# The rotation tables of a scanned state layer: GpSimd starts them behind the first norm, and VectorE makes its first pair behind the lower half of h

## The chip, the cores and the metric

The kernel runs on one core of a Trainium2 chip. The metric is the device time of one execution in microseconds (us), the median of several runs. A core has five engines with a queue each: PE (TensorE, matrix products into PSUM), DVE (VectorE), ACT (ScalarE), POOL (GpSimd), and SP (SyncE, which here issues nearly all the transfers). Each works its queue in order and waits on semaphores.

## The reference, cut to what matters

Two networks of two layers each run one after the other on x, 256 tokens by 1024 features, in float32. The change lies in the first layer of the first network: a norm, one projection that gives u (for a state-space layer) and q, k, v (for attention), and the linear recurrence over the 256 tokens.

```python
h = modulate(rms_norm(x, norm_g[layer, 0]), sh1, sc1)
proj = h @ ab_w_in[i]                 # 1024 -> 512 (u) + 3 * 512 (q, k, v)
y_ssm = s5_mixer(u, ...)              # 32 groups x 64 complex states
...
# s5_mixer: x_t = a * x_(t-1) + (B u)_t for every complex state, a = exp(lambda * dt)
_, _, xr, xi = lax.associative_scan(combine, (a_full_re, a_full_im, bu_re, bu_im), axis=1)
y = einsum(xr, c_re) - einsum(xi, c_im) + d_skip * uf
```

The kernel turns the complex recurrence into a real one: it multiplies B u by e^(-i*theta*t), runs two real scans with the magnitude of a, and multiplies by e^(i*theta*t). The cosines and sines of theta*t are the rotation tables.

## The kernel before, in words

The 32 x 64 = 2048 states lie in ST = 16 tiles of 128 partitions. The tables `e_re` and `e_im` have 16 tiles of 256 tokens each. A call of `e_pair(v, link, g)` (lines 491 to 502) makes two tiles of both, with six operations of 128x512 on engine `v`: four products and a difference and a sum, all between tiles in SBUF (two SBUF inputs each), from the small tables `e1` and `e2`. The tables have eight pairs. GpSimd makes pairs 4 to 7 (tiles 8 to 15) in its first loop (lines 725 to 728), which waits for `powers_ready` alone, that is for `e1` and `e2`. VectorE makes pair 0 behind `x_scaled(0)`, pair 1 behind the split of the third weight chunk, and pairs 2 and 3 behind tiles 2 and 4 of the scan. GpSimd's tables are first read by tile 8 of the scan, far behind: VectorE waits there for `e_ready`.

Every weight comes as a chunk of 128x2048 into one of three buffers. ACT rounds it (`w_hi`, L750), DVE makes the rest (`w_lo`, L1338), and PE multiplies three products for each pair of tiles (L2231), 48 products a chunk here. ACT's `w_hi(q)` waits for PE to have used chunk q-3; the load of chunk q waits for ACT and DVE to have split chunk q-3.

The order of work at the start, as each queue has it:

- PE: 16 pieces of the modulation's weights as they land (L2182), `x_turn(0)` (16 transposes of the scaled x into PSUM, L2105), `pm_turn(1)` (L2189), then chunk 0 of `ab_in`, which follows `h_ready` pair by pair; `bu(0)` and `bu(1)` (L2286); then for c = 1 to 7 chunk c, `bu(c+1)`, and from c = 2 on `y_of(c-2)` (L2299). `bu(j)` needs `bu_used` of tile j-2, because two banks take turns.
- DVE: `x_scaled(0)` (L1507, L1516), `e_pair` 0, `w_lo(0)`, `first_mod_out` (L1492, waits for `pm_turn(1)`), `x_gains(0)` (L1523), `x_lower(0)` (L1539, L1540; the lower half of h), `w_lo(1)` and `w_lo(2)`, `e_pair` 1; then for c = 0 to 7: `w_lo(c+3)`, `ssm_tile(c)` (L1614 to L1631).
- ACT: `w_hi(0)`, `x_upper(0)` (L792, L794, waits for the gains), `w_hi(1)`, `w_hi(2)`; then for each c the copy out of chunk c (L904) and `w_hi(c+3)`.
- SP: the pieces, chunks 0 and 1, and when all 16 pieces are used chunks 2 to 5; then, behind a wait for `h_ready` of the whole first norm, four transfers of attention biases, then chunks 6 and 7 and what follows. Behind `w_lo(10)`, the last split of this stretch, come the later pieces of the modulation.

`h_ready` is counted by `x_lower`; `H[1]` = 4 is its value when the first norm's h is complete. In a scan tile L1614 and L1615 read a PSUM bank and a table; L1617, L1618, the two scans L1620, L1629 and L1631 read SBUF alone, with two inputs each. The second of them, L1615, releases `bu_used`.

Of the kernel before, what the change touches and what calls it, by code (L numbers as in the profile page):

```python
# [255 lines left out]
def build(nc, A, out):  # L256
    with ExitStack() as ctx:
# [5 lines left out]
        def sem(name):  # L263
            if name not in names:
                names[name] = ctx.enter_context(nc.semaphore(name))
            return names[name]
# [172 lines left out]
        def chunks(name, n):  # L439
            Q[name] = sum(k for _, k in stream)  # L440
            stream.append((name, n))
# [5 lines left out]

        MB = {1: 0, 4: MOD_BLOCKS}
        NQ = sum(k for _, k in stream)

        raw_landed = [sem(f"raw_landed{i}") for i in range(SLOTS)]
# [39 lines left out]
        def e_pair(v, link, g):  # L491

            j = slice(2 * g, 2 * g + 2)
            a, b = ([e[:, i, j, :].unsqueeze(k).broadcast_to([P, 2, 16, 16]) for i in range(2)] for e, k in ((e1, 3), (e2, 2)))
            er, ei = (t[:, j, :].rearrange("p j (a b) -> p j a b", b=16) for t in (e_re, e_im))
            part = e_part[g >= E_POOL]
            v.tensor_tensor(er, a[0], b[0], ALU.mult)
            link(v.tensor_tensor(part, a[1], b[1], ALU.mult))
            link(v.tensor_tensor(er, er, part, ALU.subtract))
            v.tensor_tensor(ei, a[0], b[1], ALU.mult)  # L500
            link(v.tensor_tensor(part, a[1], b[0], ALU.mult))
            return v.tensor_tensor(ei, ei, part, ALU.add)
# [48 lines left out]
        SQ, UPPER, H, SCALES = [0], [0], [0], [0]  # L551
# [20 lines left out]
        def _(sp):  # L572
# [10 lines left out]
            def load_mod(m, i=None):  # L583

                more = 0 if i is None else 6 * i
                buf, landed, _, n = MOD_HALF[m]
                sp.wait_ge(sem("mod_used"), MOD_SLOTS + m - n + 1 + more)
                src = A["mod_stream"][bass.ds(m + more, 1)].rearrange("o p (k n) -> (o p) k n", k=DT // 2)
                sp.dma_start(buf, src).then_inc(landed, 16)
# [128 lines left out]
        @block.gpsimd  # L718
        def _(pool):
            done = Count(sem("pool_chain"))  # L720

            def link(ins):
                pool.wait_ge(done.sem, done.on(ins))

            pool.wait_ge(sem("powers_ready"), 1)
            for g in range(E_POOL, ST // 2):
                e_pair(nc.gpsimd, link, g).then_inc(sem("e_ready"), 1)
                pool.wait_ge(sem("e_ready"), g - E_POOL + 1)
            for j in range(8, ST):
                pool.wait_ge(sem("scan_done"), j - 7)  # L730
                pool.wait_ge(*((sem("state_ready"), j - 1) if j >= 10 else (sem("ssm_y_done"), j - 1)))
                nc.gpsimd.tensor_tensor(by_sin[j % 2], rot_b, e_im[:, j, :].unsqueeze(1).broadcast_to([P, 2, T]), ALU.mult)\
                    .then_inc(sem("sin_part"), 1)
            pool.wait_ge(sem("h_ready"), H[7])
            pool.wait_ge(sem("mod_turned"), 2 * MOD_BLOCKS)
            for v in (q_head, k_head):
                nc.gpsimd.memset(v[32:64, 1::2, :], 0.0).then_inc(sem("heads_zeroed"), 1)
# [588 lines left out]
        def _(dve):  # L1326
            chain = Count(sem("dve_chain"))

            def link(ins):
                dve.wait_ge(chain.sem, chain.on(ins))  # L1330
# [9 lines left out]
            def lo_upto(q):  # L1340
                while nxt[0] <= min(q, NQ - 1):
                    lo(nxt[0])
                    nxt[0] += 1
# [165 lines left out]
            def x_scaled(n):  # L1509

                if n:
                    dve.wait_ge(sem("h_ready"), H[n])
                for t in range(2):
                    x_recip(n, t)
                    for fh in range(2):
                        nc.vector.tensor_scalar(x_at(hf_tok, t, fh), x_at(x, t, fh), x_rstd[:, t:t + 1], None, ALU.mult)\  # L1516
                            .then_inc(sem("x_scaled"), 1)
# [81 lines left out]
            dve.wait_ge(sem("x_landed"), 16)  # L1599
            dve.wait_ge(sem("c_ready"), 1)  # L1600
            x_scaled(0)
            link(e_pair(nc.vector, link, 0))
            lo_upto(0)
            first_mod_out(0, 2)
            x_gains(0)
            x_lower(0)
            lo_upto(2)
            link(e_pair(nc.vector, link, 1))

            def ssm_tile(j):  # L1610
                dve.wait_ge(sem("bu_ready"), j + 1)
# [1177 lines left out]
```

## Time and profile before

| what | value |
| --- | --- |
| median of 3 runs | 1541.3 us (1537.97 to 1543.39) |
| the profiled execution | 1540.02 us, of which the span 1538.2 us |
| granted TensorE clock, mean | 0.969 |
| busy: PE, DVE, ACT, POOL | 1437.3, 1128.9, 772.6, 51.5 us |
| share of the chain that ended last: PE, DVE, ACT, DMA, issue | 73%, 12%, 5%, 5%, 4% |

The span is the profiled part of the execution; 1.8 us lie around it. The chain is followed back from the last instruction, at each step to what released it. A share of busy time is an average over the whole span; the change touches only the first 9% of it, up to some 135 us.

### The profile page before, as it was taken

What the parts mean: (1) busy time and instruction counts of PE and PEld (TensorE: products, weight loads), DVE (VectorE), ACT (ScalarE), POOL (GpSimd) and SP (SyncE); (2) the same over time, 40 slices, a digit from 0 to 9 for tenths busy, and PEclk for the clock granted to TensorE, in tenths of its full rate; (3) what the DMA queues carried; (4) which work ended last, traced back from release to release, by engine and by line L of the source; (5) the groups of instructions that cost most, each with busy time, mean ns of one, the idle gap of its engine ahead of it and who ended that gap; (6) DMA issues with size and microseconds to landing.
All of it is one profiled execution on the core that took longest, in us unless ns stands there. A gap on an engine that the chain in (4) does not pass through costs nothing.

```text
span 1538.2 us, 24906 instructions
## 1 busy us (share of the span) xinstructions
PE 1437.3 (93%) x9469; PEld 1201.6 (78%) x9483; DVE 1128.9 (73%) x1680; ACT 772.6 (50%) x1090; POOL 51.5 (3%) x38
## 2 busy tenths in 40 slices
PE   5598989999988999999999889999999999999998
PEld 1585458899966668999979755799997877799997
DVE  7999756988874465998985467586667859676666
ACT  3332356555554355555555567555455542455554
POOL 2600200000000000000001000000000000000000
PEclk9598999999989999999998999999999999999999
DMA  9332944988859944998833400455554533345551
GB/s 356 136 126 89 334 172 198 354 319 306 310 198 384 373 192 188 355 361 314 337 147 113 134 14 5 149 178 178 194 188 169 187 110 137 110 164 191 177 199 61
DMA packets 58061, 315.65 MB, mean 205 GB/s; under 512 B 7012, under 2 KB 8525, under 8 KB 33857
## 3 DMA queue, kind: packets, MB, share of 16 engines
q1 hardware_dynamic: 53826, 303.30, 53.3%
q10 hardware_dynamic: 4158, 11.30, 2.3%
q8 instruction: 52, 0.85, 0.2%
q14 instruction: 25, 0.20, 0.0%
HBM read 311.85 MB, written 1.15 MB: 203 GB/s over the span
## 4 chain that ended last, share of the span: by engine, by line
PE 73%; DVE 12%; ACT 5%; DMA 5%; issue 4%; SPq 0%; ACTq 0%; DVEq 0%; POOL 0%
PE bank L2231 61%; DMA raw<-in_stream 2%; PE bank L2490 2%; DMA arena<-in_mod_later 2%; ACT w_hi L750 1%; DVE w_lo L1338 1%; PE bank L2105 1%; DVE hf L1552 1%; DVE h_lo L1540 1%; ACT hf L1255 1%; PE bank L2299 1%; PE bank L2182 1%; PE bank L2286 1%; PE bank L2123 1%; ACT hf L792 1%
## 5 line engine op out<-in xcount | busy, mean ns | idle before, releaser
L1338 DVE TENSOR_TENSOR w_lo<-raw,w_hi 128x2048 fp32r<-128x2048 f32 x186 | 426.3, 2293 | 176.8 <-ACT w_hi L750 175.6
L2231 PE MATMUL bank<-h_hi,w_hi 128*128 128x256 f32 x1800 | 519.9, 289 | 18.3 <-DVE h_lo L1540 16.7
L2231 PE MATMUL bank<-h_lo,w_hi 128*128 128x256 f32 x1800 | 513.3, 285 | 0.0
L2231 PE MATMUL bank<-h_hi,w_lo 128*128 128x256 f32 x1800 | 513.1, 285 | 0.0
L750 ACT ACTIVATE w_hi<-raw 128x2048 fp32r<-128x2048 f32 x186 | 355.8, 1915 | 138.7 <-PE bank L2231 114.4
L2231 PEld LDWEIGHTS bank<-h_hi,w_hi 128*128 128x128 f32 x1800 | 349.4, 194 | 19.3 <-DVE h_lo L1540 9.6
L2231 PEld LDWEIGHTS bank<-h_lo,w_hi 128*128 128x128 f32 x1800 | 349.5, 194 | 2.3 <-issue 0.7
L2231 PEld LDWEIGHTS bank<-h_hi,w_lo 128*128 128x128 f32 x1800 | 349.4, 194 | 0.0
L1755 DVE SCALAR_TENSOR_TENSOR arena<-bank,par,arena 128x255 f32<-128x255 f32 (+1 forms) x264 | 109.1, 475 | 111.5 <-ACT arena L987 79.1
L2231 PE MATMUL bank<-w_hi,a_hi 128*128 128x512 f32 x368 | 146.4, 398 | 10.9 <-DVE a_lo L1780 10.1
L2231 PE MATMUL bank<-w_hi,a_lo 128*128 128x512 f32 x368 | 144.5, 393 | 0.0
L2231 PE MATMUL bank<-w_lo,a_hi 128*128 128x512 f32 x368 | 144.4, 392 | 0.0
L987 ACT ACTIVATE arena<-bank,par 128x256 f32<-128x256 f32 x88 | 44.8, 560 | 139.8 <-PE bank L2231 139.8
L1366 DVE SCALAR_TENSOR_TENSOR arena<-arena,silu_c 128x384 f32<-128x384 f32 (+1 forms) x192 | 104.3, 613 | 0.0
L2231 PE MATMUL bank<-w_hi,h_hi 128*128 128x512 f32 (+1 forms) x224 | 87.1, 389 | 5.8 <-DVE hf L1552 3.0
L2231 PEld LDWEIGHTS bank<-w_hi,a_hi 128*128 128x128 f32 x368 | 69.8, 190 | 28.1 <-DVE w_lo L1338 11.1
L2231 PE MATMUL bank<-w_hi,h_lo 128*128 128x512 f32 (+1 forms) x224 | 84.7, 378 | 0.0
L2231 PE MATMUL bank<-w_lo,h_hi 128*128 128x512 f32 (+1 forms) x224 | 84.6, 378 | 0.0
L2231 PEld LDWEIGHTS bank<-w_lo,a_hi 128*128 128x128 f32 x368 | 69.7, 189 | 15.1
L2231 PEld LDWEIGHTS bank<-w_hi,a_lo 128*128 128x128 f32 x368 | 69.9, 190 | 13.1
L1005 ACT ACTIVATE a_hi<-arena 128x512 fp32r<-128x512 f32 x44 | 27.8, 632 | 59.5 <-DVE arena L1776 59.4
L2231 PEld LDWEIGHTS bank<-w_hi,h_hi 128*128 128x128 f32 x224 | 42.7, 191 | 19.0 <-issue 11.1
(327 smaller groups left out, 1705.2 us busy)
## 6 DMA issues: line engine op xcount, KB each, us to landing
raw<-in_stream SPq DMA_DIRECT2D x186, 1024.0 KB, 5.0
arena<-in_mod_stream SPq DMA_DIRECT2D x64, 768.0 KB, 7.6
arena<-in_mod_later SPq DMA_DIRECT2D x48, 512.0 KB, 9.1
raw<-in_mod_pe SPq DMA_DIRECT2D x36, 512.0 KB, 6.3
arena<-in_mod_pe SPq DMA_DIRECT2D x12, 512.0 KB, 12.1
sq<-row_store ACTq DMA_DIRECT2D x7, 512.0 KB, 3.7
sq<-in_bias SPq DMA_DIRECT2D x8, 256.0 KB, 6.8
x<-in_x_t ACTq DMA_DIRECT2D x1, 1024.0 KB, 9.0
```

Of the source, the lines that this page charges most:

```text
L750: nc.scalar.activation(w_hi[s][:], raw[s][:], ACT.Copy).then_inc(hi_done, 1)
L792: nc.scalar.activation(hf[:, k, :], turned(n, k), ACT.Identity, **by).then_inc(sem("full_ready"), 1)
L987: ins = nc.scalar.activation(gate_c[:, e, :], half(4, e), ACT.Identity, scale=par[:, bass.ds(wb[center] + 2 * s + e, 1)], bias=par[:, bass ...
L1005: nc.scalar.activation(slot_hi(q), act_f, ACT.Copy)\
L1255: nc.scalar.activation(mla_s(h, t), bank[u % 4][:], ACT.Exp, bias=small[:, k + 1:k + 2], scale=MLA_SCALE, accum_out=small[:, k + 2:k + 3]) ...
L1338: nc.vector.tensor_tensor(w_lo[s][:], raw[s][:], w_hi[s][:].bitcast(F32), ALU.subtract).then_inc(lo_done, 1)
L1366: ins = nc.vector.scalar_tensor_tensor(parts[e], buf[:, kt % 4, :], silu_c[:, c0 + kt:c0 + kt + 1], parts[e], ALU.mult, ALU.add)
L1540: ins = nc.vector.tensor_tensor(v["parts"][1][:, k, :], hf[:, k, :], up.bitcast(F32), ALU.subtract)
L1552: ins = nc.vector.tensor_tensor(part, acc[:], row_at(gate_rows[gate], fh), ALU.mult)
L1755: ins = nc.vector.scalar_tensor_tensor(o, src, par[:, bass.ds(w[tap] + 2 * s + e, 1)], o, ALU.mult, ALU.add)
L2231: ins = nc.tensor.matmul(out_, l, r, start=first and n == 0, stop=last and n == 2, **kw)
L2490: ins = nc.tensor.matmul(bank[2 * part + ft][:], dft[:, part, t, ft * P:(ft + 1) * P], sources[part][:, t, 512 * s_:512 * s_ + 512], start ...
```

## The change

GpSimd waits for the first norm's h (`h_ready` at `H[1]`) before it begins its four pairs. VectorE's pair 0 moves from behind `x_scaled(0)` to directly ahead of pair 1, behind `x_lower(0)` and `w_lo(2)`. No operation is added or removed but GpSimd's wait.

```diff
             pool.wait_ge(sem("powers_ready"), 1)
+            pool.wait_ge(sem("h_ready"), H[1])
             for g in range(E_POOL, ST // 2):
                 e_pair(nc.gpsimd, link, g).then_inc(sem("e_ready"), 1)
...
             x_scaled(0)
-            link(e_pair(nc.vector, link, 0))
             lo_upto(0)
             first_mod_out(0, 2)
             x_gains(0)
             x_lower(0)
             lo_upto(2)
-            link(e_pair(nc.vector, link, 1))
+            for g in range(2):
+                link(e_pair(nc.vector, link, g))
```

## Rows read from the trace of the kernel before

**Rows 1.** The chain that ended last: start us, us, engine, tile, line.

```profile
69.33 8.33 PE bank L2231 x48
79.46 5.95 PE bank L2231 x48
...
123.67 5.96 PE bank L2231 x48
130.14 1.91 ACT w_hi L750
132.07 2.29 DVE w_lo L1338
```

**Rows 2.** Timeline of DVE, 30 to 63 us: start us, us, line, operation, tiles.

```profile
30.22 2.38 DVE L1516 TENSOR_SCALAR hf<-x,small 128x512 f32<-128x512 f32 x2
...
35.13 1.54 DVE L497 TENSOR_TENSOR arena<-arena 128x512 f32<-128x512 f32 x1
...
42.96 1.43 DVE L502 TENSOR_TENSOR arena<-arena 128x512 f32<-128x512 f32 x1
44.42 3.02 DVE L1338 TENSOR_TENSOR w_lo<-raw,w_hi 128x2048 fp32r<-128x2048 f32 x1
47.37 0.16 DVE L1492 TENSOR_TENSOR mod<-bank,par 128x16 f32<-128x16 f32 x1
47.56 1.02 DVE L1523 SCALAR_TENSOR_TENSOR gains<-mod,par 128x8 f32<-128x8 f32 x1
...
60.91 2.58 DVE L1540 TENSOR_TENSOR h_lo<-hf,h_hi 128x256 fp32r<-128x256 f32 x2
```

**Rows 3.** Timeline of DVE, 67 to 81 us.

```profile
67.81 0.68 DVE L497 TENSOR_TENSOR arena<-arena 128x512 f32<-128x512 f32 x1
...
71.91 2.29 DVE L1338 TENSOR_TENSOR w_lo<-raw,w_hi 128x2048 fp32r<-128x2048 f32 x1
...
74.72 0.68 DVE L1615 TENSOR_TENSOR arena<-bank,arena 128x512 f32<-128x512 f32 x1
...
78.14 0.69 DVE L1631 TENSOR_TENSOR arena<-arena 128x512 f32<-128x512 f32 x1
80.19 2.29 DVE L1338 TENSOR_TENSOR w_lo<-raw,w_hi 128x2048 fp32r<-128x2048 f32 x1 [1.36 <-ACT w_hi L750]
```

**Rows 4.** Timeline of POOL; 24 table operations from 30.07 to 63.20 us.

```profile
30.07 1.06 POOL L497 TENSOR_TENSOR arena<-arena 128x512 f32<-128x512 f32 x1 [29.61 <-DVE arena L1460]
...
45.38 3.19 POOL L502 TENSOR_TENSOR arena<-arena 128x512 f32<-128x512 f32 x1
...
61.86 1.34 POOL L502 TENSOR_TENSOR arena<-arena 128x512 f32<-128x512 f32 x1
142.56 1.71 POOL L732 TENSOR_TENSOR arena<-arena 128x512 f32<-128x512 f32 x1 [79.36 <-DVE arena L1620]
```

**Rows 5.** DVE lines over the whole span: shortest, median and longest of one in ns.

```profile
L1516 DVE TENSOR_SCALAR hf<-x,small x32: 478/485/1306, 30.2 to 1340.7; 128x512 f32<-128x512 f32 x32
L1540 DVE TENSOR_TENSOR h_lo<-hf,h_hi x64: 424/426/1501, 49.9 to 1347.2; 128x256 fp32r<-128x256 f32 x64
```

**Rows 6.** Timeline of ACT, 38 to 56 us.

```profile
48.62 1.02 ACT L792 ACTIVATE hf<-bank,mod,gains 128x256 f32<-128x256 f32 x2 [12.53 <-DVE gains L1523]
...
53.58 0.63 ACT L794 ACTIVATE h_hi<-bank,mod,gains 128x256 fp32r<-128x256 f32 x1
```

**Rows 7.** Timeline of PE, 38 to 79 us.

```profile
38.12 0.51 PE L2189 MATMUL bank<-ident_sb,arena 128*128 128x4 f32 x4
52.49 0.58 PE L2231 MATMUL bank<-h_hi,w_hi 128*128 128x256 f32 x1 [13.87 <-DVE h_lo L1540]
...
78.33 1.13 PE L2286 MATMUL bank<-arena 32*128 32x256 f32 x4 [0.69 <-ACT arena L904]
```

**Rows 8.** Windows: length, busy PE, PEld, DVE, ACT, POOL, granted clock, DMA share, GB/s.

```profile
40.00:42.00 2.00, 0.00 (x0) 0.00 (x0) 2.00 (x2) 0.00 (x0) 1.92 (x2) 0.64 0.00 0
...
74.00:75.00 1.00, 1.00 (x8) 1.00 (x8) 1.00 (x3) 0.00 (x0) 0.00 (x0) 0.66 0.99 379
```

**Rows 9.** Waits, 26 to 145 us: us in total, times, longest us.

```profile
DVE w_lo L1338 <- ACT w_hi L750: 2.8, 3, 1.4
```

## The prediction, made before the run

> **What bounds the kernel now.** I read the chain that ended last first, then the timelines of the engines for the first 145 us, then the windows for the clock, since the change touches nothing later. From 79 us on the chain is PE, chunk after chunk: chunk 2 starts at 79.46 and chunk 7 at 123.67, so 8.84 us a step, 5.95 of them the 48 products [rows 1]. Then it leaves PE for ACT's `w_hi` at 130.14 and DVE's `w_lo(10)` at 132.07 [rows 1]. Behind that split SP issues the later modulation pieces, and PE, DVE and the heads follow it, so **the start of `w_lo(10)` is the mark**: what it moves by, I take the end to move by. But DVE is hardly less loaded than PE there. One of its steps is `w_lo` and a scan tile, about 7.0 us, and behind tiles 2 and 4 it also makes a pair of tables: 74.11 to 134.28 us holds only 2.8 us of waiting for ACT [rows 9]. A DVE that arrives more than about 3 us late delays the mark.
>
> Before 79 us DVE is the bound, and it is slowed. While GpSimd makes its tables (30.07 to 63.20 us, [rows 4]) DVE's operations last longer: the scaling 1.19 us each instead of 0.485 [rows 2, 5], the lower half of h 1.29 instead of 0.426 [rows 2, 5], an operation of `e_pair` some 1.55 (pair 0 takes 35.13 to 44.42, 9.29 us, for six) against 0.68 at 67.81, where a pair takes 4.1 [rows 2, 3], a `w_lo` 3.02 against 2.29 [rows 2, 3]. The addition is nearly the same whatever the operation is: 0.7 to 0.9 us. So a DVE operation waits once for the GpSimd operation in progress, and then runs at its own speed. It holds for the tiny one too: the gains, 8 columns, take 1.02 us, while the operation just ahead of it, which reads PSUM, takes 0.16 [rows 2]. GpSimd pays in the same coin: 3.19 us for the operation that met a `w_lo` [rows 4].
>
> The Trainium skill says the same as a mechanism (SBUF — State Buffer, "SBUF: two separate sides"): the port pair shared by VectorE and GpSimd is locked by one instruction for its whole length, and only a VectorE operation with two SBUF inputs or in a two-port mode needs it. The rows agree, the 0.16 beside the 1.02 included.
>
> **The change, part by part.** *(1) GpSimd waits for all of h.* Up to there DVE runs unslowed. Scaling: four at about 0.45 and two small reciprocals, 30.0 to 32.1 us instead of 35.1, a saving of 3.0. *(2) Pair 0 is gone from there*: 9.3 us less ahead of `w_lo(0)`, which now runs 32.1 to 34.3. That is then not what ends last. `first_mod_out` needs `pm_turn(1)`, which ends at 38.63 [rows 7] behind pieces that arrive by DMA and the 16 transposes, and that is unchanged. DVE is idle for 4.3 us. The gains are ready at about 39.1 instead of 48.6. *(3) ACT's upper half* takes from 48.62 to 54.21, 5.6 us [rows 6], so 39.1 to 44.7; DVE now follows it rather than sets the pace, and h is complete at 45.2 instead of 63.5 (60.91 + 2.58, [rows 2]). That is 18.3 us earlier, and it is the last big gain.
>
> *(4) What is late next.* ACT needs 1.9 us for each of `w_hi(1)` and `w_hi(2)`: ready at 46.7 and 48.6, so DVE idles 1.5 us more. GpSimd has started at 45.2, and its 24 operations lie on what DVE does now, all of it with two SBUF inputs: `w_lo(1)` and `w_lo(2)` at 3.0 each, to 52.7; pairs 0 and 1 at 9.3 each, to 71.3; `w_lo(3)`, another 3.0, to 74.2. Tile 0's first two operations read PSUM, 1.2 us: `bu_used` of tile 0 comes at 75.4. In the trace before L1615 ended at 75.40 [rows 3]. So the 18 us are spent: 9.3 for pair 0, 5.2 for pair 1 slowed, some 2.3 for three slowed `w_lo`, 1.5 for ACT.
>
> *(5) GpSimd is not done then.* It gets one operation through for each DVE operation: about 3 by 52.7, 12 beside the pairs, 1 beside `w_lo(3)`, 1 or 2 beside the PSUM operations, so 6 or 7 are left at 75.4. Tile 0 has six more operations with two SBUF inputs, 3.4 us unslowed (75.40 to 78.83, [rows 3]). At 0.85 each they cost 5.1 more. The trace of before has no scan beside GpSimd's tables; from below it is nothing for the two scans, 3.4 in all, from above 0.9 each, 5.4. I take 5.1, since scans have two SBUF inputs as well. GpSimd ends at about 83, 50 us ahead of tile 8, the first reader, so its own delay costs nothing. Tile 0 ends at 83.8 and `w_lo(4)` starts there, against 80.19 [rows 3]: **DVE is 3.6 us late** where it had waited 1.36 us for ACT.
>
> *(6) PE.* Chunk 0 can start at 41.2. The clock falls in the 40 to 42 window (mean 0.64) after PE's last work at 38.63 [rows 7, 8], and PE does nothing different until 41.2, so chunk 0 starts at the lower level (1.2 of 2.4 GHz) and needs up to 10.3 us: done by 50 to 51.6, chunk 1 by 58 to 63. Then PE stands until `bu_used` of tile 0, 75.4, because `bu(2)` is queued ahead of chunk 2. Before, `bu(2)` was at 78.33, held by ACT's copy of chunk 1 [rows 7]. PE is thus 2.9 us ahead, but has idled for over 12 us and comes back at the lower level. Before, chunk 1 took 8.33 instead of 5.95 us with the clock rising at 74.7 [rows 1, 8]; I charge chunk 2 the same 2.4. It ends at 85.1, against 85.4: nothing won. Next `bu(3)` needs tile 1: 83.8 + 2.2 (`w_lo(4)`) + 1.3 = 87.3, where before PE had it at 85.34. So chunk 3 starts 2.0 us later than before.
>
> *(7) To the mark.* From there I follow both queues with 7.0 us for a DVE step, 4.1 for a pair, and PE's 8.84. DVE's tile 2 with pair 2 ends at 101.8, tile 3 lets `bu(5)` go at 105.3, chunk 5 starts at 108.2; tile 4 and pair 3 end at 119.8, tile 5 lets `bu(7)` go at 123.3, and chunk 7 runs 126.3 to 132.2. ACT's copy and `w_hi(10)` take 2.5 more, and `w_lo(10)` starts at 134.7, against 132.07: **+2.6 us**.
>
> Cross-check by DVE alone: GpSimd's 24 operations cost it one hold each before and after, less the two or three that now pass while DVE idles or reads PSUM (-2). It gains new idle time of 4.3 + 1.5 + some 2 at ACT's pace in `x_lower`, and loses 0.7 there and at most 2.8 later: -2 + 7.8 - 3.5 = +2.3. The same size.
>
> **Other edits** cost nothing: GpSimd's added wait is one instruction with only its own tables and the later products behind it, the first of which is at 142.56 [rows 4]. SP's bias transfers wait for `h_ready` too, but are queued behind chunk 5, whose buffer is free when `w_lo(2)` is done, 52.7; they come some 15 us earlier, beside no other load that is urgent.
>
> **Sum.** Profiled execution 1540.0 + 2.6 = 1542.6 us. The median of the runs is 1.3 above the profiled one: 1541.3 + 2.6 = **1543.9 us**.
>
> **The rivals.**
> *A, faster: the tables are not slowed, and PE keeps its lead.* If pairs 0 and 1 took 4.1 each beside GpSimd, tile 0 would come 10.4 us sooner, at 65, and PE would not idle long. DVE then works ahead and PE's 8.84 a step decides: the mark some 10 us earlier, about 1531. Against it stands pair 0 itself, 9.29 us beside GpSimd [rows 2]. It decides if an operation of a pair takes under about 1.1 us (12 times 0.45 is 5.4 us). Half of it, GpSimd finishing sooner, would give 1537 to 1539. 7 in 100 for over 0.3% faster.
> *B, slower: PE's clock.* After standing from about 60 to 75 PE may stay at the lower level for all of chunks 2 and 3. A chunk at that level takes 10.2 us instead of 5.95, so 4.3 more for each, less what I charged (2.4) : +2.6 + 6.1 = 8.7, some of it hidden because DVE is late anyway (2.0): 1548. For it: the rise at 74.7 came only 22 us after PE's restart at 52.49 [rows 7, 8], with pauses. Against it: behind 69.3 PE was busy without a pause, and the rise came 5.4 us later. It decides if the clock is not up by about 88 us. 12 in 100.
> *C, nothing: DVE's lateness is absorbed.* If tile 0 is held less (the scans free, or GpSimd done by 78), DVE is at most 1.5 us late at `w_lo(4)` and PE's 0.3 us lead shows: -0.3 to +1, 1541 to 1542. 25 in 100.
> The forecast, +1 to +4.6, has the remaining 56 in 100; its own range is 1541.5 to 1546.
>
> **Numbers.** A run of this kernel can be told from no change by about 0.3%, 4.6 us. The forecast and C lie within it; the runs themselves spread by 5 us. The range that leaves out 2 in 10: 1538 to 1549. Chances: faster 0.07, same 0.80, slower 0.13.
>
> **What would show it.** h complete at 45 instead of 63.5; gains at 39; `x_lower` at ACT's pace. GpSimd's 24 operations from 45 to about 83. Pairs 0 and 1 about 9.3 us each. PE idle from about 60 to 75, a low clock until about 81. `bu_used` of tile 0 within 1 us of 75.4, `w_lo(4)` at 83 to 84, `w_lo(10)` at 134 to 135, and from there a constant shift. Wrong if pairs take under 6 us each, if GpSimd is done before 75, or if the shift behind 135 us is not that of `w_lo(10)`.

## The result, and the profile after

The changed kernel takes 1544.8 us (median of 12 runs, 1541.6 to 1547.0). The kernel before takes 1537.7 (12 runs, 1533.9 to 1544.6, the three that the forecast started from among them). The ratio is 1.0044, 95% interval [1.0028, 1.0060]: **slower by 6.8 us** (the two medians lie 7.1 apart). A second comparison of the same two kernels, on another occasion, gave 1.0038 [1.0024, 1.0052]. The forecast was +2.6 us; the absolute time, 1543.9, came nearer than that only because the median of the kernel before is 3.6 us lower here than in those three runs.

The profiled execution of the changed kernel has a span of 1542.7 us, 4.5 more than before. The timeline of VectorE (start us, us, line, operation, tiles); lines behind the added one are higher by 1:

```profile
29.88 0.88 DVE L1517 TENSOR_SCALAR hf<-x,small 128x512 f32<-128x512 f32 x2
...
38.24 0.17 DVE L1493 TENSOR_TENSOR mod<-bank,par 128x16 f32<-128x16 f32 x1 [4.29 <-PE bank L2190]
...
44.26 0.43 DVE L1541 TENSOR_TENSOR h_lo<-hf,h_hi 128x256 fp32r<-128x256 f32 x1 [0.16 <-ACT h_hi L795]
46.05 6.30 DVE L1339 TENSOR_TENSOR w_lo<-raw,w_hi 128x2048 fp32r<-128x2048 f32 x2 [1.37 <-ACT w_hi L751]
52.28 1.54 DVE L497 TENSOR_TENSOR arena<-arena 128x512 f32<-128x512 f32 x1
...
70.78 3.02 DVE L1339 TENSOR_TENSOR w_lo<-raw,w_hi 128x2048 fp32r<-128x2048 f32 x1
...
74.32 0.67 DVE L1616 TENSOR_TENSOR arena<-bank,arena 128x512 f32<-128x512 f32 x1
...
77.56 3.06 DVE L1621 TENSOR_TENSOR_SCAN arena<-cols,arena 128x256 f32<-128x256 f32 x2
...
83.52 3.26 DVE L1339 TENSOR_TENSOR w_lo<-raw,w_hi 128x2048 fp32r<-128x2048 f32 x1
...
137.80 2.29 DVE L1339 TENSOR_TENSOR w_lo<-raw,w_hi 128x2048 fp32r<-128x2048 f32 x1 [1.00 <-ACT w_hi L751]
```

The scaling is unslowed (0.44 us each), DVE idles 4.3 us for the modulation, and h is complete at 44.7, 18.8 us earlier than before [rows 2]. Then every operation with two SBUF inputs is held: two `w_lo` take 6.30, two pairs 18.5 (52.28 to 70.78), the two scans 3.06 where two take 1.27 unslowed. L1616 reads PSUM and takes 0.67. `bu_used` of tile 0 comes at 75.0, where it was 75.4 [rows 3], and `w_lo(4)` starts at 83.52 instead of 80.19. `w_lo(10)`, the mark, starts at 137.80 instead of 132.07 [rows 1]: 5.7 us late. The timeline of GpSimd, first and last table operation:

```profile
44.83 1.06 POOL L497 TENSOR_TENSOR arena<-arena 128x512 f32<-128x512 f32 x1 [44.37 <-DVE h_lo L1541]
...
83.01 1.62 POOL L502 TENSOR_TENSOR arena<-arena 128x512 f32<-128x512 f32 x1
```

Its work took 33.1 us before [rows 4] and takes 39.8 now: it meets three `w_lo` of VectorE and two pairs in place of one `w_lo`, one pair and the shorter operations of the lower half of h, and the longer ones hold it longer (3.21 us beside a `w_lo`, 1.06 with nothing to meet). PE's timeline, where a stretch begins (with the idle time ahead of it), and two windows with the granted clock in the third column from the right:

```profile
75.14 2.04 PE L2287 MATMUL bank<-arena 32*128 32x256 f32 x4 [18.13 <-DVE arena L1616]
77.11 0.58 PE L2232 MATMUL bank<-h_hi,w_hi 128*128 128x256 f32 x1
88.03 2.07 PE L2287 MATMUL bank<-arena 32*128 32x256 f32 x4 [3.30 <-DVE arena L1616]
90.03 3.62 PE L2300 MATMUL bank<-arena 128*32 128x256 f32 x8
93.58 0.58 PE L2232 MATMUL bank<-h_hi,w_hi 128*128 128x256 f32 x1
99.90 1.12 PE L2287 MATMUL bank<-arena 32*128 32x256 f32 x4
```

```profile
80.00:82.00 2.00, 2.00 (x16) 2.00 (x15) 1.97 (x3) 0.00 (x0) 1.92 (x3) 0.80 0.00 0
88.00:90.00 2.00, 1.97 (x4) 1.16 (x4) 1.96 (x4) 0.00 (x0) 0.00 (x0) 0.50 0.70 283
94.00:96.00 2.00, 2.00 (x17) 2.00 (x17) 1.93 (x5) 0.00 (x0) 0.00 (x0) 0.89 0.51 143
```

PE stands 18.1 us ahead of `bu(2)` and 3.3 us ahead of `bu(3)`. Behind each pause it comes back at 1.2 GHz. The second fall is the one the forecast did not have: from `bu(3)` to `bu(4)` it takes 11.87 us (88.03 to 99.90), where a step is 8.84 [rows 1]. The difference is 3.0 us.

Why is the span only 4.5 us longer, with a mark 5.7 late? The same split compared in both traces lies 6.2 us later at 343 us of the trace before, 7.5 at 600 and 769, and 4.1 at 870. Near 845 us the trace of before happens to have a low clock that the changed kernel's trace lacks. Window of before first, then of after, 842 to 846:

```profile
842.00:846.00 4.00, 4.00 (x21) 4.00 (x20) 3.57 (x5) 0.38 (x1) 1.92 (x1) 0.50 0.51 160
```

```profile
842.00:846.00 4.00, 3.42 (x31) 3.34 (x29) 2.25 (x7) 1.17 (x4) 0.45 (x1) 1.00 0.51 213
```

The change is not the reason: the second trace of the changed kernel loses the same 2.8 us of its lateness there, and of all eleven traces other than that of before ten gain 1.4 to 2.8 us on it; the eleventh (both pauses filled) has a low clock there too, 0.58 from 846 to 850 us. So the medians are the better measure of the end, and the mark the better measure of the change.

### The profile page after: what moved, and what is told of

Read it like the earlier page. It is cut to its first block, busy times and chain, and to the rows that moved or that the text cites. A ratio compares the mean times of both kernels' runs of the same rounds, so it can differ in the third digit from the quotient of the medians.

```text
span 1542.7 us, 24920 instructions
## 1 busy us (share of the span) xinstructions
PE 1433.9 (93%) x9483; PEld 1196.4 (78%) x9483; DVE 1128.5 (73%) x1680; ACT 772.5 (50%) x1090; POOL 58.2 (4%) x38
## 4 chain that ended last, share of the span: by engine, by line
PE 74%; DVE 10%; DMA 6%; ACT 5%; issue 4%; SPq 0%; ACTq 0%; DVEq 0%; POOL 0%
PE bank L2232 60%; DMA raw<-in_stream 2%; DVE w_lo L1339 2%; DMA raw<-in_mod_pe 2%; DMA arena<-in_mod_later 2%; PE bank L2491 2%; ACT w_hi L751 2%; PE bank L2106 1%; PE bank L2183 1%; PE bank L2124 1%; PE bank L2300 1%; ACT hf L793 1%; PE bank L2575 1%; PE bank L2287 1%; DVE small L1976 1%
## 5 line engine op out<-in xcount | busy, mean ns | idle before, releaser
L2232 PE MATMUL bank<-w_lo,h_hi 128*128 128x512 f32 (+1 forms) x224 | 85.1, 380 | 0.0
```

Source lines behind the costliest of these rows:

```text
L2232: ins = nc.tensor.matmul(out_, l, r, start=first and n == 0, stop=last and n == 2, **kw)
```

## The experiments

All eight variants change only the first 200 us. Beside the mark, the start of `w_lo(10)`, I read the time from the start of `w_lo(3)` to it, because executions differ by up to 2 us in when the first transfers land. Ratios are to the kernel before, timed beside each of them; before's median was 1537.7 to 1538.4 each time.

| kernel | `w_lo(3)` | `w_lo(10)` | between | median us | ratio, 95% interval |
| --- | --- | --- | --- | --- | --- |
| before | 71.91 | 132.07 | 60.16 | 1537.7 | 1 |
| changed | 70.78 | 137.80 | 67.02 | 1544.8 | 1.0044 [1.0028, 1.0060] |
| changed, again | 71.58 | 138.76 | 67.18 | 1543.2 | 1.0038 [1.0024, 1.0052] |
| GpSimd's wait alone | 61.75 | 133.32 | 71.57 | 1537.8 | 0.9998 [0.9983, 1.0014] |
| pair 0 moved alone | 72.71 | 133.47 | 60.76 | 1538.6 | 1.0000 [0.9981, 1.0019] |
| changed, 12 products | 70.35 | 135.03 | 64.68 | 1543.6 | 1.0037 [1.0022, 1.0052] |
| the same, again | 72.49 | 137.18 | 64.69 | 1541.8 | 1.0025 [1.0011, 1.0039] |
| changed, both pauses filled | 71.43 | 136.10 | 64.67 | 1542.4 | 1.0024 [1.0009, 1.0038] |
| changed, no GpSimd tables | 60.03 | 120.11 | 60.08 | 1526.4 | 0.9920 [0.9892, 0.9948] |
| wait alone, products in the pauses | 61.93 | 130.67 | 68.74 | 1541.3 | 1.0026 [1.0013, 1.0040] |
| wait, pairs 6 and 7 late | 62.03 | 122.32 | 60.29 | 1530.8 | 0.9957 [0.9941, 0.9973] |
| no wait, pairs 6 and 7 late | 64.21 | 123.05 | 58.84 | 1529.7 | 0.9951 [0.9933, 0.9969] |

### GpSimd's wait alone

```diff
             pool.wait_ge(sem("powers_ready"), 1)
+            pool.wait_ge(sem("h_ready"), H[1])
             for g in range(E_POOL, ST // 2):
```

> One half of the change: GpSimd waits for all of h, but VectorE's pair 0 stays behind the scaling, ahead of w_lo(0). Theory (the table operations of the two engines hold each other once per operation, and VectorE's queue is the bound until tile 0): pair 0 now runs unslowed, about 4.1 us, in the hole that the changed kernel has from 34 to 38 us, so it is free; the gains stay at 38.5 us and h is complete at 44.6 us. Only pair 1 is made beside GpSimd, so tile 0 releases its bank at about 65 us instead of 74.9, and GpSimd's remaining operations slow tile 0 and tile 1. The start of w_lo(10) comes at about 130 us, against 132.1 in the kernel before and 137.8 in the changed one: 2 us faster than before. Rival (the whole loss comes from GpSimd's late start, whatever VectorE does): w_lo(10) stays at 136 to 138 us and the kernel is as slow as the changed one.

Pair 0 was free as expected: it runs unslowed from 31.73, the gains are at 38.59, and tile 0 comes 9 us earlier than in the changed kernel. But no gain is left at the end. VectorE, then PE, of this variant:

```profile
31.73 0.68 DVE L497 TENSOR_TENSOR arena<-arena 128x512 f32<-128x512 f32 x1
...
74.50 3.26 DVE L1339 TENSOR_TENSOR w_lo<-raw,w_hi 128x2048 fp32r<-128x2048 f32 x1
...
86.47 2.29 DVE L1339 TENSOR_TENSOR w_lo<-raw,w_hi 128x2048 fp32r<-128x2048 f32 x1
...
133.32 2.29 DVE L1339 TENSOR_TENSOR w_lo<-raw,w_hi 128x2048 fp32r<-128x2048 f32 x1 [1.33 <-ACT w_hi L751]
```

```profile
79.01 2.07 PE L2287 MATMUL bank<-arena 32*128 32x256 f32 x4 [3.71 <-DVE arena L1616]
...
101.09 1.67 PE L2287 MATMUL bank<-arena 32*128 32x256 f32 x4 [1.69 <-DVE arena L1616]
102.68 3.62 PE L2300 MATMUL bank<-arena 128*32 128x256 f32 x8
```

The holds have moved to tiles 0 and 1 (12.0 us from `w_lo(4)` to `w_lo(5)` instead of 7), and PE comes back twice at the low clock, at `bu(3)` behind a pause of 3.7 us and at `bu(5)` behind one of 1.7. The rival, that all of the loss comes from GpSimd's late start, falls: the late start with pair 0 left in place is no slower than before.

### Pair 0 moved alone

```diff
             x_scaled(0)
-            link(e_pair(nc.vector, link, 0))
             lo_upto(0)
...
-            link(e_pair(nc.vector, link, 1))
+            for g in range(2):
+                link(e_pair(nc.vector, link, g))
```

> The other half: pair 0 behind w_lo(2), but GpSimd starts at 30 us as before. Theory: the scaling, w_lo(0) and the lower half of h are slowed by GpSimd (h complete at about 54 us), and the two pairs run mostly unslowed, GpSimd being done at about 62 us, so tile 0 releases its bank at about 72 to 73 us against 75.4 before; w_lo(10) at 129 to 131 us, 1 to 3 us faster than before. Rival (moving pair 0 behind h is what costs): w_lo(10) later than the 132.1 of before, at 134 to 138.

Neither is right. GpSimd ended at 66.0, four us later than expected, so it slowed `w_lo(1)`, `w_lo(2)` and three of pair 0's six operations too, and `w_lo(3)` came at 72.71, no earlier than before. The mark, 133.47, is 1.4 us later, just short of the rival's range, and the median says no change. PE, then VectorE:

```profile
76.35 2.04 PE L2286 MATMUL bank<-arena 32*128 32x256 f32 x4 [6.55 <-DVE arena L1615]
...
86.74 1.12 PE L2286 MATMUL bank<-arena 32*128 32x256 f32 x4
```

```profile
89.34 2.29 DVE L1338 TENSOR_TENSOR w_lo<-raw,w_hi 128x2048 fp32r<-128x2048 f32 x1 [2.75 <-ACT w_hi L750]
```

The 1.4 us are PE's. It stood 6.6 us ahead of `bu(2)`, came back at the lower clock (0.50 from 74 to 83 us) and began `bu(3)` at 86.74, where it was 85.34 before. VectorE, 0.5 us ahead at `w_lo(4)` (79.67), then had to wait. Here the slow chunk 2 does count, because VectorE does not hold `bu(3)`. This is read from one trace; no run filled this pause.

So in the median **each half alone is neutral, and only the two together are slower**: with both, pair 0 leaves the time in which VectorE would otherwise stand, and both pairs meet GpSimd.

### The changed kernel with 12 products of zeros behind chunk 2, twice

```diff
+                if c == 2:
+                    stay_awake(12)
                 bu(c + 1)
```

> The changed kernel with 12 products of zeros into an unused bank between chunk 2 and bu(3), where TensorE stands from 84.7 to 88.0 us and comes back at the lower clock. Theory (the clock's second fall costs 3 us of the loss): granted clock 1.00 from 82 us on, bu(3), y_of(0) and chunk 3 at 1.1, 1.9 and 5.95 us instead of 2.1, 3.6 and 6.3, w_lo(10) at about 134.8 us instead of 137.8, so 3 us faster than the changed kernel and 2 to 4 slower than before. Rival (VectorE alone sets the mark): w_lo(10) within 1 us of 137.8.

```profile
84.17 2.54 PE L2124 MATMUL bank<-zeros 128*128 128x512 bf16 x11
87.61 1.13 PE L2287 MATMUL bank<-arena 32*128 32x256 f32 x4 [0.91 <-DVE arena L1616]
88.67 1.91 PE L2300 MATMUL bank<-arena 128*32 128x256 f32 x8
```

(One of the twelve products is missing from these rows.) The clock stays up (1.00 from 84 to 96 us), `bu(3)` and the products for y take 1.13 and 1.91 us again, and the time between the two splits shrinks by 2.3, from 67.0 to 64.7. The median moved less, by 1.1, so I ran it beside the changed kernel:

> The changed kernel once more, unchanged, beside the two others of this call: 5.5 to 8 us slower than the kernel before in the median, w_lo(10) at 137 to 138.5 us. What its span adds to or takes from that behind 600 us should differ from the first profile's, if that difference (3.4 us near 850 us) was one of execution and not of the change.

> The changed kernel with 12 products of zeros behind chunk 2, once more and on the same chip as the changed kernel. Theory (the second fall of the clock costs 2.8 us at the mark and the end follows the mark): median 2 to 3.5 us below the changed kernel of this call. Rival (the products are paid back later, where the clock falls at other places): within 1.5 us of it.

1543.2 and 1541.8 us: 1.4 apart, with intervals that overlap, and on the rival's side of the line (within 1.5). The price of the second fall ahead of the mark is shown: the time between the splits is 2.3 and 2.5 us shorter without it. That it reaches the end in full is not. The split at 343 us of the trace before lay 4.4 and 2.3 us late in these two traces, and 6.2 and 3.8 in the first two, so the attention heads between take up or add some 2 us from one execution to the next. The changed kernel's 5.1 over before is also a little under the 5.5 that I expected, its mark, 138.76, a little above the 138.5, and what its trace gains on that of before near 850 us did not differ from the first one's, as I had expected it to.

### Both pauses filled

```diff
+                if c in {1: 78, 2: 28}:
+                    stay_awake({1: 78, 2: 28}[c])
                 bu(c + 1)
```

> The changed kernel with products of zeros in both pauses: 78 behind chunk 1 and 28 behind chunk 2. Theory (VectorE holds bu(3) until 88 us anyway, so the slow chunk 2 cost nothing): granted clock 1.00 from 60 to 100 us, chunk 2 ends near 82 us instead of 84.7, w_lo(10) within 0.7 us of the 135.0 that the products behind chunk 2 alone gave. Rival (each fall of the clock costs its full price): w_lo(10) at 132 to 133 us.

```profile
60.00:96.00 36.00, 34.54 (x195) 21.20 (x193) 35.48 (x31) 2.40 (x2) 24.45 (x16) 1.00 0.19 63
```

With the clock at 1.00 for the whole stretch, the time between the splits is 64.67, against 64.68 with the second pause alone filled. (The mark itself, 136.10, is 1.1 later than 135.03, as `w_lo(3)` is already; that is outside the 0.7 I had given.) So in the changed kernel the slow chunk 2 costs nothing: VectorE holds `bu(3)` until 88 us whatever PE does.

### The changed kernel without GpSimd's tables

```diff
+            for g in range(E_POOL, ST // 2):
+                nc.gpsimd.memset(e_re[:, 2 * g:2 * g + 2, :], 1.0)
+                nc.gpsimd.memset(e_im[:, 2 * g:2 * g + 2, :], 0.0).then_inc(sem("e_ready"), 1)
+            pool.wait_ge(sem("e_ready"), 4)
             pool.wait_ge(sem("powers_ready"), 1)
             pool.wait_ge(sem("h_ready"), H[1])
-            for g in range(E_POOL, ST // 2):
-                e_pair(nc.gpsimd, link, g).then_inc(sem("e_ready"), 1)
-                pool.wait_ge(sem("e_ready"), g - E_POOL + 1)
```

> The changed kernel without GpSimd's 24 table operations: its tables are filled with constants at the start instead (this part of the computation is left out). Theory (one hold of 0.7 to 0.9 us for each GpSimd operation): pairs 0 and 1 take 4.1 us each, tile 0 releases its bank at 62 us instead of 74.9, w_lo(10) at 118 to 121 us, so 17 to 20 us faster than the changed kernel. Rival (the pairs are slow for another reason, or TensorE alone sets the mark from there): less than 10 us faster.

```profile
47.41 4.49 DVE L1340 TENSOR_TENSOR w_lo<-raw,w_hi 128x2048 fp32r<-128x2048 f32 x2 [1.38 <-ACT w_hi L752]
51.82 0.68 DVE L497 TENSOR_TENSOR arena<-arena 128x512 f32<-128x512 f32 x1
...
66.99 2.29 DVE L1340 TENSOR_TENSOR w_lo<-raw,w_hi 128x2048 fp32r<-128x2048 f32 x1
```

The pairs take 4.1 us each. From `w_lo(1)` to `w_lo(4)` VectorE needs 19.6 us (47.41 to 66.99) instead of 37.5 (46.05 to 83.52). That is 17.9 us, for the 21 operations with two SBUF inputs that VectorE has in that stretch (three `w_lo`, two pairs, six of tile 0): 0.85 us each. The median is 18.4 us below the changed kernel, and 12 below before.

### GpSimd's wait alone, with products of zeros in its pauses

The edit is against GpSimd's wait alone.

```diff
+                if c in {1: 38, 2: 14, 4: 6}:
+                    stay_awake({1: 38, 2: 14, 4: 6}[c])
                 bu(c + 1)
```

> GpSimd's wait alone (pair 0 left where it was), with TensorE kept busy by products of zeros where it stood in that variant: 38 behind chunk 1, 14 behind chunk 2, 6 behind chunk 4. Theory (in the variant without them the clock fell twice, at bu(3) and bu(5), and TensorE then set the mark at 133.3 us): with the clock up VectorE alone is the bound, w_lo(10) starts at 129.5 to 130.5 us, 2 us ahead of the kernel before, and the median is 1 to 3 us below the kernel before. Rival (the products of zeros delay bu, or VectorE waits for ACT as much as before): w_lo(10) at 132 to 134 us.

```profile
79.19 1.13 PE L2287 MATMUL bank<-arena 32*128 32x256 f32 x4 [2.75 <-DVE arena L1616]
...
82.89 0.58 PE L2232 MATMUL bank<-h_hi,w_hi 128*128 128x256 f32 x1
```

The mark came at 130.67, 2.65 us ahead of the variant without the products, close to what the theory said. Its condition held in part only: the 14 products left a pause of 2.75 us ahead of `bu(3)`, and the clock fell behind it all the same (0.80 from 80 to 82 us, 0.50 to 84). The median did not follow: 1541.3 us, 3.5 above that variant, with intervals that just meet. The profiled execution was one of the fastest, 1537.6. Its split at 343 us of the trace before lies 3.1 us early and the one at 612 lies 1.7 late; between them the clock was low where it was not without the products (0.87 from 480 to 490 us and 0.88 from 560 to 570, against 1.00 in both windows for GpSimd's wait alone). Whether the products cause this, one trace each can't tell; why most executions are longer is left open.

### Half of GpSimd's tables made among the heads

```diff
-            for g in range(E_POOL, ST // 2):
+            for g in range(E_POOL, E_POOL + 2):
                 e_pair(nc.gpsimd, link, g).then_inc(sem("e_ready"), 1)
...
                     .then_inc(sem("sin_part"), 1)
+                if j < 12:
+                    g, which = E_POOL + 2 + (j - 8) // 2, j % 2
+                    ins = e_pair(nc.gpsimd, link, g, which)
+                    if which:
+                        ins.then_inc(sem("e_ready"), 1)
+                        pool.wait_ge(sem("e_ready"), g - E_POOL + 1)
+                    else:
+                        link(ins)
```

`which` picks a half of the pair's six operations, first the three for `e_re`, then the three for `e_im`; tiles 12 to 15 get their tables so. This stands on the variant with GpSimd's wait and pair 0 in its old place.

> GpSimd's wait alone, and of its four pairs only 4 and 5 made at once; pairs 6 and 7 are made in halves behind its products of tiles 8 to 11. Theory (each of GpSimd's operations takes 0.7 to 0.9 us from VectorE while VectorE is the bound, and less among the attention heads, where VectorE waits for TensorE 10 us in all): GpSimd is done with the first two pairs at about 66 us, tile 0 and tile 1 run unslowed, w_lo(10) starts at 121 to 124 us, some 10 us ahead of the variant without this, and about half of that is given back among the heads: the median 4 to 9 us below the kernel before. Rival (what is taken out of the first part comes back whole among the heads): median within 2 us of the kernel before.

```profile
62.03 3.02 DVE L1351 TENSOR_TENSOR w_lo<-raw,w_hi 128x2048 fp32r<-128x2048 f32 x1
...
70.60 2.29 DVE L1351 TENSOR_TENSOR w_lo<-raw,w_hi 128x2048 fp32r<-128x2048 f32 x1
...
122.32 2.29 DVE L1351 TENSOR_TENSOR w_lo<-raw,w_hi 128x2048 fp32r<-128x2048 f32 x1 [0.67 <-ACT w_hi L763]
```

The mark is 9.8 us earlier than before, as expected. I had expected half to be given back among the heads; the splits behind them lie 10.4 to 10.5 us earlier than before, so nothing was. The median is 7.3 us below before. The same without GpSimd's wait:

> Pairs 6 and 7 in halves among the heads as before, but GpSimd begins its first two pairs at 30 us, without the wait for h. Theory (what matters is how many table operations meet a VectorE that is the bound, not where they begin): GpSimd is done at about 46 us, the scaling, pair 0 and w_lo(0) are slowed as in the kernel before, the lower half of h hardly; h is complete near 54 us, tile 0 releases its bank at 66 to 67 us, about as with the wait (65.9), and w_lo(10) starts at 121 to 125 us; the median 5 to 9 us below the kernel before. Rival (GpSimd's wait is what gains): 3 us or more slower than with the wait.

```profile
53.90 0.42 DVE L1552 TENSOR_TENSOR h_lo<-hf,h_hi 128x256 fp32r<-128x256 f32 x1 [0.15 <-ACT h_hi L806]
...
64.21 2.29 DVE L1350 TENSOR_TENSOR w_lo<-raw,w_hi 128x2048 fp32r<-128x2048 f32 x1
...
123.05 2.29 DVE L1350 TENSOR_TENSOR w_lo<-raw,w_hi 128x2048 fp32r<-128x2048 f32 x1 [0.64 <-ACT w_hi L762]
```

h is complete at 54.3, 9.2 us later than with the wait, and the mark is only 0.7 later; the medians, 1530.8 and 1529.7, can't be told apart. So with pair 0 in its old place it does not matter much where GpSimd begins. It matters how many of its operations meet VectorE while VectorE is the bound. (With pair 0 moved it does matter: the changed kernel differs from pair 0 moved alone by GpSimd's wait only, and takes 6 us more.) Both versions beat both kernels, by 0.4 to 0.5% against before.

## Why the prediction was right and where it fell short

The direction and the mechanism were right, the size was not: +2.6 us were forecast, with +1 to +4.6 as the forecast's own range, and +6.8 [+4.3, +9.2] were measured. I had given a loss of over 0.3% only 13 in 100, and both comparisons came out at 0.38 and 0.44%. That 1544.8 us lies within 0.9 of the 1543.9 forecast is luck: the starting value was 3.6 us too high.

- **Parts 1 to 3** held. Gains at 38.6 (39.1 forecast), h complete at 44.7 (45.2).
- **Part 4** held: `bu_used` of tile 0 at 75.0 (75.4), the pairs 9.3 and 9.2 us. The run without GpSimd's tables shows that it is GpSimd that slows them. That all 18 us of the early h are spent before tile 0 is the heart of the result.
- **Part 5** held, in its upper half: scans are held like the rest, 0.9 us each. `w_lo(4)` began at 83.52 (83.8). GpSimd ended at 84.6, not 83, and so met that split as well: 3.26 us instead of 2.29. `bu(3)` was let go at 88.03 (87.3).
- **Part 6** is **the step that failed**. I charged the low clock once, at chunk 2, where it cost nothing: filling that pause as well changed 64.68 to 64.67. And I let PE run chunk 3 at full clock behind a 3.3 us pause, where the clock fell a second time and cost PE 3.0 us, of which 2.3 and 2.5 show in the time between the splits. The forecast had a pause of 2.2 us there in its own numbers: chunk 2 done at 85.1, `bu(3)` at 87.3. The rows of before have a low clock within two to three us of PE's last work (0.64 from 40 to 42, after 38.63) [rows 7, 8]; I did not carry it over. With the second fall filled the mark is at 135.03, where I had 134.7. 134.7 + 3.0 is 137.7 and 137.80 was measured, but the second trace has 138.76, so the agreement to 0.1 is partly luck. Rival B named a slow chunk 3 and its price, but as one long fall and not as a second one.
- This explains the mark and not the whole of the end. Without the second fall the medians are still 5.3 and 3.7 us above before, where I had forecast 2.6; they fell by 1.1 and 1.4 only, within the noise. What makes up the rest of the loss in the medians stays open.
- Chunk 0 ran at full clock here (PE back at 40.63, after 2.2 us), not at the lower level as forecast; in the second trace of the same kernel the clock fell in it. Nothing hung on it.
- **Part 7**, the constant shift behind the mark, holds within 2 us: 6.2 us at 343 us of the trace before, 7.5 at 600. The last 1.1 between the mark and the median's 6.8 lies in this scatter and is not assigned.
- **Rival A** fell: a pair beside GpSimd took 9.2 us, not 4.1. **Rival C** fell with the scans.
- The Trainium skill's page (SBUF — State Buffer, "SBUF: two separate sides") has the shared port locked by one instruction for its length. The traces agree: GpSimd's operations beside a `w_lo` took 3.21, 2.99 and 3.10 us, those with a free port 1.06, and VectorE's PSUM reads of tile 0, made while GpSimd was at work, were not held (0.68 and 0.67).

## What to carry to other kernels

Where two engines hold each other once per operation, moving one engine's work later moves the holds and does not remove them; put it where the other engine is not the bound, as pairs 6 and 7 among the heads: that saved 7 us. Operations that lie in a wait of their own engine are free; look for what fills such a gap before moving work out of it, as pair 0 did. And when a sum leaves the matrix engine a pause of two or three us, give the fall of the clock behind it a chance and a price, but only for work that then sets the end: the slow chunk 2 was free in the changed kernel, where VectorE held the next step, and not with pair 0 moved alone.

## What the hardware showed that I had not expected

- GpSimd's six operations of a pair took 9.2 us beside VectorE's operations of the same size, and so did VectorE's: the two run in strict turns. With nothing to meet, one of GpSimd's took 1.06 us.
- Scans (two SBUF inputs, 128x256) are held like products: 1.53 us each instead of 0.64.
- The length of a pause did not tell whether the clock falls. Chunk 0 of the changed kernel follows a pause of 2.20 us in both traces. In the first the clock stayed at 1.00 through chunk 0 and fell in chunk 1, with PE busy, after a further pause of 1.8 us (0.52 from 50 to 52 us); in the second it fell in chunk 0. The window from 42 to 44 us, first trace, then second:

```profile
42.00:44.00 2.00, 2.00 (x19) 2.00 (x19) 1.74 (x5) 2.00 (x5) 0.00 (x0) 1.00 0.07 29
```

```profile
42.00:44.00 2.00, 2.00 (x11) 2.00 (x11) 1.61 (x5) 2.00 (x6) 0.00 (x0) 0.50 0.05 21
```

- Behind pauses of 3.3 us (changed), 3.7 (GpSimd's wait alone) and 2.75 (the same with products) the clock fell each time, and behind one of 1.7 us ahead of `bu(5)` too (0.77 from 101 to 102 us, then 0.50).
- Twelve products of zeros keep the clock up and take 2.3 and 2.5 us out of the time between the splits, yet the median gained 1.1 to 1.4; in another variant, with 58, it lost 3.5. Two of the four traces with such products have a low clock at 560 to 570 us (0.88 and 0.83) and none of those without; that the products bring it about is not shown.
